# 30 of 34 token tiles transposed by VectorE and placed by transfers instead of TensorE transposes, in a hybrid FFN/convolution layer

## The chip, the cores and the metric

The kernel runs on the 8 cores of one Trainium2 chip. Each core computes one row of the batch (2048 prompt tokens) and 16 of the 128 sample tokens; the cores do not exchange data. The metric is the device time of the slowest core, in microseconds. Every row below is from core 0, the slowest one of the profiled execution.

## What is computed

One layer: a half-step SwiGLU feed-forward, a token mixer of two convolution groups, and a second half-step feed-forward, each followed by a layer norm.

```python
D_MODEL = 1024; SEQ = 2048; D_FF = 2816; K_A = 31; K_B = 3; D_IN = 5 * 512

def swiglu(x, w_gate, w_up, w_down):
    return (jax.nn.silu(x @ w_gate) * (x @ w_up)) @ w_down

x = layer_norm(ALPHA * x + 0.5 * swiglu(x, f1_wg, f1_wu, f1_wd), ln_f1_g, ln_f1_b)
z = x @ w_in + b_in
a_val, a_gate, g_b, g_c, b_val = jnp.split(z, 5, axis=-1)
ua = silu(layer_norm(causal_depthwise(a_val * sigmoid(a_gate), w_dw_a) + b_dw_a, ...))   # width 31
ub = g_b * causal_depthwise(g_c * b_val, w_dw_b)                                          # width 3
m = jnp.concatenate([ua, ub], axis=-1) @ w_o + b_o
x = layer_norm(ALPHA * x + m, ln_mix_g, ln_mix_b)
x = layer_norm(ALPHA * x + 0.5 * swiglu(x, f2_wg, f2_wu, f2_wd), ln_f2_g, ln_f2_b)
```

## The kernel before, in words

**Tiles and blocks.** The tokens lie in 17 tiles: 16 of 128 prompt tokens, and tile 16 with the 16 sample tokens. Tiles 0 to 7 are block 0, tiles 8 to 15 and 16 are block 1. The residual stream is token-major: a tile is 128 partitions (tokens) by 1024 features in f32, in one of the slots of `xr`, and it is spilled to DRAM between stages (`x1s` after the first feed-forward, `x2s` after the mixer). The input of a matmul that contracts over features must be feature-major: it lies in bf16 in `xA` (block 0) and `xB` (block 1), and `xcol(k, tok0, n)` is the 128 features of chunk k (of KC = 8) for n tokens. In the kernel before, tokens lie behind each other within a chunk.

**Stages.** `up` multiplies a block by gate and up weights: for each of 22 chunks of hidden width and each group of 512 (block 0) or 352 and 336 (block 1) tokens, `u_group` issues 16 matmuls (L563), ScalarE takes the silu into `sg`, and VectorE multiplies (L570) into `hT`. `down` works tile by tile: 44 matmuls (L627) from `hT`, then the residual and the layer norm on VectorE (L460 to L492) with a little GpSimd work in between. The mixer of a block is an in-projection (L720), gates (L782, L817), convolution (L838), and two units of four tiles (`unit_E`), each with a layer norm, an out-projection (L1003), the residual and the second layer norm. The program runs up(0, block 0), down(0, block 0), then up(0, block 1) merged with the mixer of block 0, down(0, block 1), up(1, block 0) merged with the mixer of block 1, down(1, block 0), up(1, block 1), down(1, block 1). In the merged stages `merge` takes the up groups as filler: after each piece of the mixer it issues as many up groups as the piece's number says, in an order fixed by these numbers.

**From token-major to feature-major.** When a tile's layer norm is done, its bf16 form stands in `xb` (2 slots). `xpose` transposes it: 8 matmuls of 128 x 128 against an identity (L438), a PSUM bank, and one copy by ScalarE (L442) into `xA` or `xB`. This happens 34 times: 17 times in `down(0, .)` for the mixer's input and 17 times in the units for the second feed-forward's.

```python
while len(pend) > (1 if late is None else 0) and not final:
    xpose(*pend.pop(0), tb())
```

**Queues and dependencies.** `Prog` (its class stands at L44 to L172) records each operation on its engine in program order, with what it reads and writes, and derives semaphore waits from these. Each engine's queue is in order, SyncE's too. SyncE issues the stores and loads of `xr` (`store_xr` L539, `load_xr` L419), the DRAM hops of the convolution (`uscr`, L799) and little else; GpSimd issues the weights (wgu, wd, win). `load_xr` reads, beside its source, what `gate[0]` names:

```python
gate = [()]
def load_xr(t, src, rtok=()):
    rtok = list(rtok) + list(gate[0])
    s = xrr()
    n = tok(t)[1]
    P.op("sp", lambda e: e.dma_start(out=xr[:n, s, :], in_=src), reads=list(rtok), writes=[("xr", s)],
         dma="xr_ld%d" % s)
```

From `down(0, block 0)` on the gate is `[("hT", 17, 1)]`: each load counts as a reader of that part of `hT`, so it waits for its last write, and its next write (by the multiply of chunk 17, group 1, of the following `up`) waits for all the loads issued before it.

## Time and profile before

| what | value |
|---|---|
| median of 3 runs | 1196.04 us (1195.96 to 1196.07) |
| the profiled execution's own time | 1196.45 us |
| its span, core 0 | 1194.9 us (cores 1192.1 to 1194.9) |
| granted TensorE clock | full in every slice |
| TensorE busy | 1179.9 us, 99% |
| VectorE busy | 599.8 us, 50% |
| ScalarE, GpSimd busy | 249.3 us (21%), 191.5 us (16%) |
| DMA | 155.92 MB, software queue 42.3% and hardware queue 22.7% of the 16 engines |

The stages of the profiled execution, in us from the span's start, with the busy time of TensorE and VectorE:

| stretch | stage | TensorE | VectorE |
|---|---|---|---|
| 0 to 170 | up(0, block 0) | 165.6 | 43.8 |
| 170 to 247 | down(0, block 0) | 77.0 | 46.0 |
| 247 to 521 | up(0, block 1) and mixer of block 0 | 272.7 | 161.2 |
| 521 to 603 | down(0, block 1) | 82.0 | 53.1 |
| 603 to 876 | up(1, block 0) and mixer of block 1 | 272.0 | 165.4 |
| 876 to 1195 | the second feed-forward's rest | 310.7 | 130.2 |

The span is the time between the first and the last record on the core; the execution's own time holds what lies around it. A busy share is an average over stages with different limits. A row with [x <-y] says that the engine stood x us before it and that y released it.

### The profile page before, as it was taken

Reading aid. Unit: us, or ns where it says so; the run is one execution under the profiler, and the core shown is the slowest. Engines: PE = TensorE matmul, PEld = TensorE weight load, DVE = VectorE, ACT = ScalarE, POOL = GpSimd, SP = SyncE. Lnnn points to the kernel's source line nnn. Section 1 sums busy time; section 2 is a strip of 40 time slices with the busy share of each in tenths; the row PEclk is TensorE's granted clock in tenths of the full one; section 3 lists DMA queues with packets and bytes.
Section 4 is the critical chain, followed back from the end, with each engine's and each line's share of the span. In section 5 each row is a group of like instructions: output and inputs, shape, how many; then the busy total and the mean of one; then the engine's idle time right before and its main releaser. Section 6 shows DMA issues by size and latency. Waiting matters only on the chain.

```text
span 1194.9 us, 20175 instructions; the slowest of 8 cores (1192.1 to 1194.9 us)
## 1 busy us (share of the span) xinstructions
PE 1179.9 (99%) x7240; PEld 644.0 (54%) x7240; DVE 599.8 (50%) x918; ACT 249.3 (21%) x451; POOL 191.5 (16%) x302
## 2 busy tenths in 40 slices
...
GB/s 281 114 211 139 142 143 152 150 153 121 120 102 112 131 129 165 200 184 124 105 114 117 114 108 125 120 135 185 185 163 136 76 107 86 71 72 89 28 105 105
DMA packets 70898, 155.92 MB, mean 130 GB/s; under 512 B 8912, under 2 KB 30608, under 8 KB 69760
## 3 DMA queue, kind: packets, MB, share of 16 engines
q0 software_dynamic: 31040, 76.07, 42.3%
q1 hardware_dynamic: 39760, 78.56, 22.7%
...
## 4 chain that ended last, share of the span: by engine, by line
PE 95%; DMA 2%; DVE 1%; issue 0%; ACT 0%; DVEq 0%; POOL 0%; SPq 0%; POOLq 0%; ACTq 0%
PE ps L563 50%; PE ps L627 25%; PE ps L720 11%; PE ps L1003 4%; PE ps L838 1%; DMA sb_xr<-x1s 1%; PE ps L438 1%; DMA sb_RW<-wgu 1%; PE ps L645 1%; PE ps L972 1%; PE ps L944 1%; DVE sb_RW L782 0%; PE ps L633 0%; DVE sb_RW L817 0%; DVE sb_ring L1179 0%
## 5 line engine op out<-in xcount | busy, mean ns | idle before, releaser
L563 PE MATMUL ps<-sb_xB,sb_ring 128*128 128x352 bf16 (+1 forms) x2112 | 319.6, 310 | 0.0
L563 PE MATMUL ps<-sb_xA,sb_ring 128*128 128x512 bf16 (+1 forms) x1472 | 311.6, 370 | 2.0 <-DVE sb_ring L1179 2.0
L570 DVE TENSOR_TENSOR sb_hT<-sb_sg,ps 128x352 bf16<-128x352 f32 (+3 forms) x224 | 129.6, 579 | 348.9 <-PE ps L563 323.3
L627 PE MATMUL ps<-sb_RW,sb_hT 128*128 128x512 bf16 x1364 | 297.0, 379 | 0.0
L563 PEld LDWEIGHTS ps<-sb_xB,sb_ring 128*128 128x128 bf16 x2112 | 205.8, 98 | 106.7 <-issue 1.1
L563 PEld LDWEIGHTS ps<-sb_xA,sb_ring 128*128 128x128 bf16 x1472 | 142.9, 98 | 156.9 <-issue 4.5
L627 PEld LDWEIGHTS ps<-sb_RW,sb_hT 128*128 128x128 bf16 x1364 | 132.9, 98 | 158.1 <-issue 0.2
L568 ACT ACTIVATE sb_sg<-ps 128x352 f32<-128x352 f32 (+3 forms) x224 | 113.8, 508 | 489.2 <-PE ps L563 454.0
L376 POOL DMA_DIRECT2D sb_ring<-wgu x84 | 46.6, 555 | 463.2 <-PE ps L563 406.7
L460 DVE SCALAR_TENSOR_TENSOR sb_xr<-sb_xr,ps 128x1024 f32<-128x1024 f32 x47 | 57.3, 1218 | 94.2 <-PE ps L627 77.0
L468 POOL TENSOR_SCALAR sb_mv<-sb_mv 128x1 f32<-128x1 f32 (+1 forms) x50 | 43.5, 869 | 354.4 <-DVE sb_mv L466 347.3
L720 PE MATMUL ps<-sb_xB,sb_wring 128*128 128x512 bf16 (+2 forms) x480 | 73.8, 310 | 0.5 <-DVE sb_RW L782 0.4
L720 PE MATMUL ps<-sb_xA,sb_wring 128*128 128x512 bf16 x320 | 73.0, 379 | 0.0
L464 DVE BATCH_NORM_STATS2 sb_stt<-sb_xr 128x6 f32<-128x512 f32 (+1 forms) x100 | 64.3, 685 | 5.1
L720 PEld LDWEIGHTS ps<-sb_xB,sb_wring 128*128 128x128 bf16 x480 | 46.7, 98 | 26.6 <-issue 1.6
L479 DVE SCALAR_TENSOR_TENSOR sb_xr<-sb_xr,sb_mv,sb_lnb 128x1024 f32<-128x1024 f32 (+1 forms) x33 | 42.4, 1284 | 18.5 <-POOL sb_mv L470 16.0
L720 PEld LDWEIGHTS ps<-sb_xA,sb_wring 128*128 128x128 bf16 x320 | 31.3, 98 | 34.4
L782 DVE SCALAR_TENSOR_TENSOR sb_RW<-ps,sb_cst,sb_RW 128x512 bf16<-128x512 f32 (+2 forms) x24 | 41.7, 1779 | 7.0 <-PE ps L720 5.9
L817 DVE SCALAR_TENSOR_TENSOR sb_RW<-ps,sb_cst,sb_RW 128x512 bf16<-128x512 f32 (+1 forms) x20 | 39.8, 2069 | 7.2 <-PE ps L720 7.1
L476 DVE SCALAR_TENSOR_TENSOR sb_xr<-sb_xr,sb_mv,sb_lnb 128x1024 f32<-128x1024 f32 (+1 forms) x33 | 42.2, 1280 | 1.7
L389 POOL DMA_DIRECT2D sb_wring<-win x40 | 22.0, 553 | 121.2 <-PE ps L720 119.8
L442 ACT ACTIVATE sb_xB<-ps 128x1024 bf16<-128x1024 bf16 (+1 forms) x18 | 16.8, 941 | 114.3 <-PE ps L438 114.2
...
## 6 DMA issues: line engine op xcount, KB each, us to landing
sb_ring<-wgu POOLq DMA_DIRECT2D x84, 512.0 KB, 8.1
sb_RW<-wd POOLq DMA_DIRECT2D x33, 512.0 KB, 11.1
...
sb_RW<-uscr SPq DMA_DIRECT2D x128, 67.0 KB, 5.5
sb_xr<-xp SPq DMA_DIRECT2D x16, 512.0 KB, 9.4
x1s<-sb_xr SPq DMA_DIRECT2D x16, 512.0 KB, 4.0
sb_xr<-x1s SPq DMA_DIRECT2D x16, 512.0 KB, 11.5
x2s<-sb_xr SPq DMA_DIRECT2D x16, 512.0 KB, 8.0
```

The lines of the kernel that those rows point to most:

```text
L376: P.op("pool", lambda e, q=q: e.dma_start(out=ring[:, s, q * m:(q + 1) * m], in_=wgu[w][f][:, q * m:(q + 1) * m], max_dma_last_dim=8192), ...
L460: P.op("dve", lambda e: e.scalar_tensor_tensor(out=xr[:n, s, :], in0=xr[:n, s, :], scalar=in_scale, in1=add, op0=ALU.mult, op1=ALU.add), r ...
L464: P.op("dve", lambda e, h=h: e.bn_stats(out=stt[:n, m, h, :], in_=xr[:n, s, h * 512:(h + 1) * 512]), reads=[("xr", s)], writes=[("stt", m, ...
L468: P.op("pool", lambda e: e.tensor_scalar(out=mv[:n, m, 3:4], in0=mv[:n, m, 1:2], scalar1=eps, scalar2=None, op0=ALU.add), reads=[("mv", m) ...
L476: P.op("dve", lambda e: e.scalar_tensor_tensor(out=xr[:n, s, :], in0=xr[:n, s, :], scalar=mv[:n, m, 0:1], in1=lnb[:n, 0, :], op0=ALU.subtr ...
L479: P.op("dve", lambda e: e.scalar_tensor_tensor(out=xr[:n, s, :], in0=xr[:n, s, :], scalar=mv[:n, m, 2:3], in1=lnb[:n, 1, :], op0=ALU.mult, ...
L563: ins = e.matmul(bank(bk, n), lhsT=ring[:, s, c:c + 128], rhs=xcol(k, tok0, n), start=(k == 0), stop=(k == KC - 1))
L568: P.op("act", lambda e: e.activation(out=sg[:, q, :n], in_=bank(bg, n), func=AF.Silu), reads=pst(bg), writes=[("sg", q)])
L570: P.op("dve", lambda e: e.tensor_tensor(out=hT[:, f, l0:l0 + n], in0=sg[:, q, :n], in1=bank(bu, n), op=ALU.mult), reads=[("sg", q)] + pst( ...
L627: ins = e.matmul(ps[:n, (yb + h) * 512:(yb + h + 1) * 512], lhsT=hT[:, f, l0:l0 + n], rhs=wd[:, f, h * 512:(h + 1) * 512], start=(f == 0), ...
L720: ins = e.matmul(bank(bk, n), lhsT=wring[:, slot, k * 128:(k + 1) * 128], rhs=xcol(k, tok0, n), start=(k == 0), stop=(k == KC - 1))
L1003: ins = e.matmul(ps[:n, (4 + h) * 512:(5 + h) * 512], lhsT=lhs(k), rhs=wo[:, k, h * 512:(h + 1) * 512], start=(k == 4), stop=(k == 3))
```

## The change

Of the 34 transposes, 30 go another way: tiles 0 to 6 and 8 to 14 in `down(0, .)`, and the 16 prompt tiles in the units. The last prompt tile of each block in `down(0, .)` and tile 16 (twice) keep `xpose` (L434 in the new file). For the 30:

- VectorE transposes the tile in blocks of 32 x 32 (L447), all 128 blocks in one instruction, from `xb` to `tq` (2 slots). After that each 32 x 32 block is transposed within itself, but stands on the partitions it came from.
- SyncE issues four writes from `tq` to `xscr` in DRAM (L451; 64 KB each, 4 slots of `xscr`), which put the blocks into the right rows. A write moves pieces of 512 bytes.
- `land_moves`, called later in the order, issues one transfer from `xscr` into `xA` or `xB` (L454; 256 KB in rows of 2 KB), which waits for the four writes.

For pieces of 512 bytes the feature-major buffers have another layout: runs of 16 tokens, and within a run of tokens the 8 feature chunks. A matmul's moving operand so becomes runs of 32 bytes, 256 bytes apart. The host's `xta` and `xtb` are laid out in that way. In `down`, a tile's transposes no longer stand between two tiles' matmuls. `dynamic_dma_scratch_size=8192` gives the software queue's descriptors less room than before.

```diff
-    nc = bass.Bass("TRN2", target_bir_lowering=False)
+    nc = bass.Bass("TRN2", target_bir_lowering=False, dynamic_dma_scratch_size=8192)
+    xscr = nc.dram_tensor("xscr", [4, 128, D], BF16).ap()
-        xA = sb("xA", [128, 4, KC, 256], BF16)
-        xB = sb("xB", [128, KC, NTOK - BLK], BF16)
+        xA = sb("xA", [128, KC * BLK], BF16)
+        xB = sb("xB", [128, KC * (NTOK - BLK)], BF16)
+        tq = sb("tq", [128, 2, D], BF16)
+        def xall(tok0, n):
+            (buf, o) = (xA, tok0) if tok0 < BLK else (xB, tok0 - BLK)
+            return buf[:, o * KC:(o + n) * KC]
+
         def xcol(k, tok0, n):
...
+            return xall(tok0, n).rearrange("p (b k l) -> p k b l", k=KC, l=16)[:, k, :, :]
+        moves = []
+
+        def xmove(t, c):
+            s, d = tqr(), xsr()
+            P.op("dve", lambda e: e.transpose(out=tq[:, s, :].rearrange("p (q h k l) -> p k q h l", q=4, h=2, k=KC),
+                                              in_=xb[:, c, :].rearrange("p (k q h l) -> p k q h l", q=4, h=2, k=KC)),
+                 reads=[("xb", c)], writes=[("tq", s)])
+            for a in range(4):
+                P.op("sp", lambda e, a=a: e.dma_start(out=xscr[d].rearrange("(q i) (a c) -> a i q c", q=4, a=4)[a],
+                                                      in_=tq[32 * a:32 * a + 32, s, :].rearrange("i (q c) -> i q c", q=4)),
+                     reads=[("tq", s)], writes=[("xscr", d, a)], dma="xw%d_%d" % (s, a))
+            moves.append(lambda: P.op("sp", lambda e: e.dma_start(out=xall(t * 128, 128), in_=xscr[d]),
+                                      reads=[("xscr", d, a) for a in range(4)], writes=[("xT", t)], dma="xm%d" % d))
+
+        def land_moves():
+            while moves:
+                moves.pop(0)()
@@ down
-                while len(pend) > (1 if late is None else 0) and not final:
+                land_moves()
+                while pend:
                     xpose(*pend.pop(0), tb())
...
+                        if t < 16 and i < len(tl) - 1:
+                            xmove(t, c)
+                            return []
+                        return [(t, c)]
@@ unit_E, B(i)
+                land_moves()
                 for k in at(i, 5, True):
-                    xpose(tl[k], xbs[k], ((3, 3, 3, 7), (3, 6, 3, 7))[par][k])
+                    xmove(tl[k], xbs[k])
```

Three places of the order, in which a number behind x counts equal neighbours and "waits" names what an instruction waits for. First TensorE in `down(0, block 0)`, before. Rows of L627 are the down matmuls, rows of L438 a tile's transposes.

```order
L627 MATMUL ps<-sb_RW,sb_hT 128x512 x132
L438 MATMUL ps<-sb_ident_bf,sb_xb 128x128 x8
L627 MATMUL ps<-sb_RW,sb_hT 128x512 x44
L438 MATMUL ps<-sb_ident_bf,sb_xb 128x128 x8
L627 MATMUL ps<-sb_RW,sb_hT 128x512 x44
L438 MATMUL ps<-sb_ident_bf,sb_xb 128x128 x8
```

The same place after, where L641 are the down matmuls, L577 the up matmuls, L738 the in-projection and L434 the transposes:

```order
L641 MATMUL ps<-sb_RW,sb_hT 128x512 x352
L577 MATMUL ps<-sb_xB,sb_ring 128x352 x32
L577 MATMUL ps<-sb_xB,sb_ring 128x336 x16
L738 MATMUL ps<-sb_xA,sb_wring 128x512 x16
L577 MATMUL ps<-sb_xB,sb_ring 128x352 x16
L434 MATMUL ps<-sb_ident_bf,sb_xb 128x128 x8
```

The 352 matmuls of the eight tiles now follow each other with nothing between, and only tile 7's transposes are left, behind the first piece of the in-projection.

Second, SyncE's queue in the first unit of the mixer of block 1, before. L539 is a store of a finished tile (two rows of the same store instruction read alike), L419 a load of the next tile's x1s; `xr_st1` is the store that frees slot 1.

```order
L539 DMA x2s<-sb_xr 128x1024 [waits S_dve] x2
L419 DMA sb_xr<-x1s 128x1024 [waits xr_st0]
L539 DMA x2s<-sb_xr 128x1024 [waits S_dve] x2
L419 DMA sb_xr<-x1s 128x1024 [waits xr_st1,S_act]
L419 DMA sb_xr<-x1s 128x1024 [waits xr_st2,S_act]
```

The same place after. L553 and L415 are that store and that load, L451 the writes to `xscr` (the four of a tile are a row and its "x3"), L454 the transfer from `xscr`; `xw1_0` to `xw1_3` are the four writes from slot 1 of `tq`.

```order
L553 DMA x2s<-sb_xr 128x1024 [waits S_dve]
L415 DMA sb_xr<-x1s 128x1024 [waits xr_st1,S_act]
L454 DMA sb_xB<-xscr 128x1024 [waits xw1_0,xw1_1,xw1_2,xw1_3]
L451 DMA xscr<-sb_tq 32x4x256 [waits xm0,S_dve]
L451 DMA xscr<-sb_tq 32x4x256 x3
L454 DMA sb_xB<-xscr 128x1024 [waits xw0_0,xw0_1,xw0_2,xw0_3]
L451 DMA xscr<-sb_tq 32x4x256 [waits xm1,S_dve]
L451 DMA xscr<-sb_tq 32x4x256 x3
L415 DMA sb_xr<-x1s 128x1024 [waits xr_st2,S_act]
```

The load into slot 2, which stood directly behind the one into slot 1, now has two transfers from `xscr`, each with its wait for writes, and two tiles' writes between.

Third, VectorE at that place, before: L570 is the multiply of an up group, L918 to L921 are statistics of the convolution's layer norm.

```order
L570 TENSOR_TENSOR sb_hT<-sb_sg,ps 128x512 [waits S_act,S_pe] x4
L918 BN_STATS sb_sttc<-ps 128x6 [waits S_pe]
L919 BN_AGGR sb_mvc<-sb_sttc 128x2 [waits S_dve]
L921 TENSOR_SCALAR sb_mvc<-sb_mvc 128x1 [waits S_dve]
L570 TENSOR_TENSOR sb_hT<-sb_sg,ps 128x512 [waits xr_ld0,xr_ld1,xr_ld2,S_act,S_pe]
```

After, where L584 is that multiply and L447 the block transpose:

```order
L584 TENSOR_TENSOR sb_hT<-sb_sg,ps 128x512 [waits S_act,S_pe] x2
L447 STREAM_TRANSPOSE sb_tq<-sb_xb 128x8x8x16 [waits xw0_0,xw0_1,xw0_2,xw0_3]
L584 TENSOR_TENSOR sb_hT<-sb_sg,ps 128x512 [waits S_act,S_pe]
L447 STREAM_TRANSPOSE sb_tq<-sb_xb 128x8x8x16 [waits xw1_0,xw1_1,xw1_2,xw1_3]
L584 TENSOR_TENSOR sb_hT<-sb_sg,ps 128x512 [waits S_act,S_pe]
...
L584 TENSOR_TENSOR sb_hT<-sb_sg,ps 128x512 [waits xr_ld0,xr_ld1,xr_ld2,S_act,S_pe]
```

Two block transposes now stand between the multiplies, each waiting for the writes of the tile two before it, and the multiply that waits for the three loads is still there.

## Rows read from the trace of the kernel before

**Rows 1.** The page: busy time by engine; the last chain by engine and by line.

```profile
PE 1179.9 (99%) x7240; PEld 644.0 (54%) x7240; DVE 599.8 (50%) x918; ACT 249.3 (21%) x451; POOL 191.5 (16%) x302
...
PE 95%; DMA 2%; DVE 1%; issue 0%; ACT 0%; DVEq 0%; POOL 0%; SPq 0%; POOLq 0%; ACTq 0%
PE ps L563 50%; PE ps L627 25%; PE ps L720 11%; PE ps L1003 4%; PE ps L838 1%; DMA sb_xr<-x1s 1%; PE ps L438 1%; DMA sb_RW<-wgu 1%; PE ps L645 1%; PE ps L972 1%; PE ps L944 1%; DVE sb_RW L782 0%; PE ps L633 0%; DVE sb_RW L817 0%; DVE sb_ring L1179 0%
```

**Rows 2.** The last chain in order of time: start, duration (us), engine, line, count.

```profile
197.67 9.50 PE ps L627 x44
...
207.61 9.50 PE ps L627 x44
```

**Rows 3.** Groups by form, whole run: xcount | busy us, mean ns | idle before, releaser.

```profile
L438 PE MATMUL ps<-sb_ident_bf,sb_xb 128*128 128x128 bf16 x256 | 19.2, 219 | 0.0
...
L489 DVE SCALAR_TENSOR_TENSOR sb_xb<-sb_xr,sb_mv,sb_lnb 128x1024 bf16<-128x1024 f32 x16 | 20.5, 1284 | 13.6 <-POOL sb_mv L470 13.3 <-DVE sb_xr L486 0.3
...
L782 DVE SCALAR_TENSOR_TENSOR sb_RW<-ps,sb_cst,sb_RW 128x512 bf16<-128x512 f32 x12 | 30.5, 2541 | 6.1 <-PE ps L720 5.9
...
L1179 DVE CAST sb_xA<-sb_RW 128x1024 bf16<-128x1024 f32 x3 | 2.1, 691 | 6.8 <-DMA sb_RW<-xta 6.8
```

**Rows 4.** Timeline, mixer of block 0: start, duration (us), engine, line, operation.

```profile
461.52 16.70 SPq L419 DMA_DIRECT2D sb_xr<-x1s  x3
...
476.71 0.52 DVE L570 TENSOR_TENSOR sb_hT<-sb_sg,ps 128x352 bf16<-128x352 f32 x1 [7.61 <-DMA sb_xr<-x1s]
...
478.19 2.55 PE L563 MATMUL ps<-sb_xB,sb_ring 128*128 128x352 bf16 x16
```

**Rows 5.** Line L419 (loads of x1s), 814.5 to 820 and 834 to 836.

```profile
L419 SPq DMA_DIRECT2D sb_xr<-x1s x2: 635/977/1319, 814.1 to 815.6; - x2
...
DMA to landing us min/median/max: 15.4/17.0/18.6
...
L419 SPq DMA_DIRECT2D sb_xr<-x1s x1: 320/320/320, 835.2 to 835.2; - x1
...
DMA to landing us min/median/max: 10.7/10.7/10.7
```

**Rows 6.** Timeline, mixer of block 1, first unit.

```profile
806.03 0.61 PE L438 MATMUL ps<-sb_ident_bf,sb_xb 128*128 128x128 bf16 x8
...
821.62 0.61 PE L438 MATMUL ps<-sb_ident_bf,sb_xb 128*128 128x128 bf16 x8
...
834.18 3.62 PE L563 MATMUL ps<-sb_xA,sb_ring 128*128 128x512 bf16 x16
...
834.40 0.69 DVE L570 TENSOR_TENSOR sb_hT<-sb_sg,ps 128x512 bf16<-128x512 f32 x1 [4.90 <-PE ps L972]
```

**Rows 7.** Timeline of VectorE, down(0, block 1): the first instruction of two tiles.

```profile
545.71 1.21 DVE L460 SCALAR_TENSOR_TENSOR sb_xr<-sb_xr,ps 128x1024 f32<-128x1024 f32 x1
...
553.50 1.21 DVE L460 SCALAR_TENSOR_TENSOR sb_xr<-sb_xr,ps 128x1024 f32<-128x1024 f32 x1
```

**Rows 8.** Line L799 (loads from uscr): whole run, 312 to 320, 620 to 628.

```profile
L799 SPq DMA_DIRECT2D sb_RW<-uscr x128: 302/432/1665, 270.2 to 740.9; - x128
...
DMA to landing us min/median/max: 2.9/2.9/2.9
...
DMA to landing us min/median/max: 7.2/8.2/9.2
```

**Rows 9.** Queues, 460 to 470, then 806 to 812: packets, MB, share of 16 engines.

```profile
q0 software_dynamic: 474, 1.17, 86.3%
q1 hardware_dynamic: 150, 0.56, 16.1%
...
q0 software_dynamic: 324, 0.80, 82.5%
q1 hardware_dynamic: 6, 0.02, 0.7%
...
x2s<-sb_xr SPq DMA_DIRECT2D x1, 512.0 KB, 8.4
```

More of the change, by code:

```diff
@@ L325, in build_nc @@
         xbr = Rot(range(2))
+        tqr = Rot(range(2))
+        xsr = Rot(range(4))
         mvr = Rot(range(4))
@@ L346, in xtoks @@
             return [("xT", t) for t in range(NT) if tok(t)[0] < tok0 + n and tok(t)[0] + tok(t)[1] > tok0]
+        def xall(tok0, n):
+            (buf, o) = (xA, tok0) if tok0 < BLK else (xB, tok0 - BLK)
+            return buf[:, o * KC:(o + n) * KC]
         def xcol(k, tok0, n):
-            if tok0 >= BLK:
-                return xB[:, k, tok0 - BLK:tok0 - BLK + n]
-            (p, o) = divmod(tok0, 256)
-            if o + n <= 256:
-                return xA[:, p, k, o:o + n]
-            assert o == 0 and n == 512
-            return xA[:, p:p + 2, k, :]
-        def xall(tok0, n):
-            if tok0 >= BLK:
-                return xB[:, :, tok0 - BLK:tok0 - BLK + n]
-            (p, o) = divmod(tok0, 256)
-            return xA[:, p, :, o:o + n]
+            return xall(tok0, n).rearrange("p (b k l) -> p k b l", k=KC, l=16)[:, k, :, :]
         RMS = ["RMC", "RM5", "RM6", "RM7", "RM8"]
@@ L442, in xpose_from @@
             P.op("act", lambda e: e.activation(
-                out=xall(tok0, n),
-                in_=psb[:, bk * 1024: bk * 1024 + KC * n].rearrange("p (k n) -> p k n", k=KC), func=AF.Identity),
+                out=xall(tok0, n).rearrange("p (b k l) -> p k b l", k=KC, l=16),
+                in_=psb[:, bk * 1024: bk * 1024 + KC * n].rearrange("p (k b l) -> p k b l", k=KC, l=16), func=AF.Identity),
                 reads=pst(bk), writes=[("xT", t)])
+        moves = []
[13 more added lines that the diff above has]
+                moves.pop(0)()
         def quarter_gather(bk):
@@ L685, in fin_tail @@
                         store_xr(t, slots[i], prow(yp, t) if t < 16 else ys[:, :])
-                        return None
+                        return []
                 if t == 16:
@@ L692, in down @@
                     ctx = ln_head(t, slots[i], pairs[i], in_scale, eps)
-                    return pend, lambda: pend.append(fin_tail(i, ctx))
-                pend.append(fin(i))
+                    return pend, lambda: pend.extend(fin_tail(i, ctx))
+                pend.extend(fin(i))
                 if late is not None:
-                    pend.append(fin(*late))
+                    pend.extend(fin(*late))
                     late = None
@@ L1116, in four @@
             def four():
+                land_moves()
                 n = len(ub.items)
@@ L1156, in fetch_xt @@
             t0, n, src = (BLK + 512 * j, 512, xtb[j]) if j < 2 else (SEQ, NS, xts)
-            P.op("pool", lambda e: e.dma_start(out=xall(t0, n), in_=src.rearrange("p (k n) -> p k n", k=KC)),
+            P.op("pool", lambda e: e.dma_start(out=xall(t0, n), in_=src),
                  writes=xtoks(t0, n), dma="xt%d" % j)
@@ L1184, in build_nc @@
         for i in range(4):
-            first.append(staged(2 * i, xta[i], xA[:, i, :, :].rearrange("p k n -> p (k n)"),
+            first.append(staged(2 * i, xta[i], xall(256 * i, 256),
                    (["xTh%d" % i], xtoks(256 * i, 256))))
```

5 lines of the change are left out of this document (2 added, 3 removed).

## The prediction

> **What bounds the kernel now.** I read the page first: TensorE is busy 1179.9 of 1194.9 us and holds 95% of the chain that ended last [rows 1]. So what leaves TensorE's queue shortens the run, as long as nothing else becomes late, and what makes TensorE wait lengthens it at once. The chain in order of time shows what a tile's transposes cost between two tiles of a down projection: the 44 matmuls start at 197.67 and last 9.50 us, the next 44 start at 207.61, so 0.44 us lie between [rows 2]. The groups by form give 219 ns for one such transpose [rows 3], but they overlap; eight of them take 0.44 us of the path.
>
> Then I asked where TensorE's cover is thin, and read the timelines of the two mixers. In the mixer of block 0 VectorE stood 7.61 us in front of one multiply (476.71) until a load of x1s landed [rows 4]; this load had been issued at 461.52. The load does not feed the multiply. `load_xr` names hT (17,1) as read (`gate`), so the next write of hT (17,1) waits for all loads issued before it. The reader is to see that TensorE took its next up group at 478.19, right behind. The mixer of block 1 has the same place: two loads issued at 814.1 and 815.6 landed within 18.6 us [rows 5], the later one at 834.2, and the multiply started at 834.40, while TensorE had begun the next group at 834.18 [rows 6]. (The row puts the wait down to PE; the load's landing fits to 0.2 us.) The second half of this group, 1.8 us on at 836.0, is what needs the bank, and the multiply ended at 835.1: slack 0.9 us. Whatever makes these two loads later than that stops VectorE and then TensorE.
>
> **What the change removes.** 30 of 34 tiles lose their 8 transposes: 30 x 0.44 = 13.2 us off TensorE's path [rows 2], 14 tiles in the down projections (6.2 us) and 16 in the mixers (7.0 us). ScalarE's eviction goes too; ScalarE is not on the path [rows 1], nothing counted. Fewer bytes per partition for the software queue's descriptors, the new layout of the loads and the changed source of the x transfers: nothing, bounds below.
>
> **What it adds on VectorE.** One block transpose per tile, 128x1024 bf16 with 32-byte runs out. The trace has none. Nearest rows: a cast of as many elements, 0.69 us; a plain pass over 1024, 1.28; a write with a step of two elements, 2.54 for 512, so 5.1 for 1024 [rows 3]. The runs are 16 elements long, nearer to the plain pass; I take 1.2. In a down projection VectorE needs 7.8 us for a tile (545.71 to 553.50) [rows 7] and would need 9.0, while TensorE takes 9.5: hidden, and it stays hidden up to 1.7 us. The Trainium skill (VectorE: DVE Perf Modes, "The three transpose paths") gives 311 ns for 128x128 bf16 on VectorE; eight of these would be an estimated 2.5 us. No row shows one.
>
> **What it adds on SyncE and the queues.** Per tile four writes to xscr (W, 512 packets of 512 B, 0.25 MB) and, after they have landed, one transfer back (M, 0.25 MB). SyncE's queue is in order. M waits for W, and the next tile's W, the stores and the loads stand behind M. An issue takes 0.43 us [rows 8], so W costs 1.7. How long W takes to land from its last issue, L, no row shows. Nearest are the 67 KB loads from uscr, 536-byte packets too: 2.9 us at best, 7.2 to 9.2 at worst [rows 8]. The rows of the queues say which end to take: while the software queue held 82.5% and 86.3% of the engines (wd and wgu loads), the hardware queue moved 6 packets in 6 us and 150 in 10 us [rows 9]. These are stretches of the two mixers. I take L = 7, range 2.9 to 9.2. The Trainium skill (DMA: Bandwidth & Descriptors, "Queues, rings and completion order") says that an engine goes round-robin between the rows it has work for. By that rule W would get its turn soon and L would be near its low end; the 6 packets of [rows 9] speak against it, since a store of 512 KB was issued in that stretch and took 8.4 us to land.
>
> In the down projections a tile comes every 9.5 us, L + 1.7 + 0.4 = 9.1, and nothing there waits on xT soon: no cost.
>
> Mixer of block 1, first unit. The four tiles come within 15.6 us (806.03 to 821.62) [rows 6], and SyncE would need 3 x 9.1 = 27.3. In the new order W, M, W, M, W, M, W stand before the load into slot 2. From 806.0: W1 out 807.7, M1 814.7, W2 out 816.8, M2 823.8, W3 out 825.9, M3 832.9, W4 out 835.0, then the load at 835, which was issued at 815.6. A load issued at 835.2 landed in 10.7 us [rows 5], so it lands at 845.7 instead of 834.2: 11.5 late, less 0.9 slack: 10.6. Three of the removed transposes lie inside this chain and give nothing: 1.3. **Loss 11.9.**
>
> Mixer of block 0, first unit. Only W1, M1, W2 stand ahead of the load; SyncE gets to it about 1.8 us later than 461.52 (W2's issues). But 0.5 MB more are in the queue ahead of it, and that queue moved 0.56 MB in 10 us [rows 9]: between 0 and 9 us, I take 5. 6.8 late, less 1.0 slack (the multiply ended at 477.2, TensorE went on at 478.19 [rows 4]), plus 1.3 of savings within: **loss 7.1.**
>
> The second units end without such a gate. Their last tiles come about as close together as the first unit's, two of them some 4 us apart, and each transpose waits for the W of two tiles before (tq has 2 slots), which stands behind an M: VectorE stands some 9.1 - 4 = 5 us, of which I let free banks cover 2 to 3. Bounds 0 to 5; I take 3 for block 0, 1 for block 1 (one up group is left there).
>
> **Sum**: -13.2 + 11.9 + 7.1 + 3 + 1 = +9.8 us. The profiled execution took 1196.45 (span 1194.9), the median is 1196.04, 0.4 less; so 1206. With L at 2.9 and no more queueing the load in block 1 goes out at 806.0 + 3 x 5.0 + 1.7 = 822.7 and lands, with 10.7, at 833.4, in time; the other terms shrink to 2: 1185. With L at 9.2 it goes out at 841.6 and lands with 18.6 at 860, 26 late; 9 + 1.8 in block 0; 6 for the rest: about 1225.
>
> **Rivals.** (1) *The gain stays*: W lands within 3 to 4 us, TensorE keeps its cover, 1185 to 1193. For it: the 2.9 us of [rows 8], and stores that the stalled TensorE's software queue makes room for. Against: [rows 9]. It decides at L about 4.5, where the losses are 13. By the skill's round-robin rule this is the case. Chance 0.26. (2) *They cancel* within 0.2% (2.4 us, about what a measurement tells from no change): 0.08. (3) *VectorE becomes the bound*: at 2.5 us a tile needs 10.3 against 9.5, 14 x 0.8 = 11 us on top of the stalls, about 1217; at 5.1 us 14 x 3.4 = 48, over 1240. Or the 32-byte runs slow the up matmuls: L563 and L720 hold 61% of the chain [rows 1], so 2% would be 15 us. No row has a moving operand in short runs. Together 0.09. (4) *The change does nothing* is out: the transposes leave the queue. (5) The forecast, SyncE's order and the gate cost more than the transposes: 0.57.
>
> Slower 0.57 + 0.09 = 0.66, same 0.08, faster 0.26. The range 1187 to 1220 leaves out the best half of the first rival's low end and the worst of the bound cases; the forecast's own range is 1199 to 1220.
>
> **What would show it.** Right: 32 transposes left on PE; 30 on VectorE of 1.0 to 1.6 us; W landing in 6 to 9 us in the mixers; SyncE waiting on DMA xscr some 7 us each; a wait of VectorE's multiply on the load of x1s of over 12 us in each mixer, and idle time of TensorE near it, about 10 us in block 1. Down projections at 9.50 us a tile without gaps. Wrong: up matmuls longer than before in the same form; W landing in under 4.5 us; TensorE's idle in the mixers unchanged.

## The result

The changed kernel is slower: 1241.54 us against 1196.05, ratio 1.038 with a 95% interval of 1.0348 to 1.0413. Times of whole kernels are medians of the executions in which no die showed a lower clock (here three, 1238.55 to 1244.77; a fourth took 1270.33). The prediction had slower as the likeliest case, but said 1206 with a range of 1187 to 1220, and the result lies above it. The profiled execution took 1241.54 us with a span of 1240.0 on its slowest core.

The page of the kernel after: busy time, and the last chain by engine and by line, as in [rows 1].

```profile
PE 1180.8 (95%) x7000; PEld 634.0 (51%) x7000; DVE 633.6 (51%) x948; ACT 220.4 (18%) x421; POOL 186.7 (15%) x302
...
PE 81%; DMA 10%; DVE 4%; SPq 2%; issue 2%; POOL 1%; DVEq 0%; ACT 0%; POOLq 0%; ACTq 0%
PE ps L577 44%; PE ps L641 19%; PE ps L738 10%; DMA xscr<-sb_tq 6%; PE ps L1021 4%; DMA sb_xr<-x1s 2%; PE ps L856 1%; SPq L451 1%; DMA sb_RW<-xta 1%; DVE sb_xr L474 1%; PE ps L659 1%; DVE sb_stt L478 1%; DVE sb_tq L447 1%; POOL sb_mv L482 1%; DVE sb_xb L503 1%
...
L447 DVE STREAM_TRANSPOSE sb_tq<-sb_xb 128x1024 bf16<-128x1024 bf16 x30 | 37.2, 1239 | 30.0 <-DMA xscr<-sb_tq 30.0
```

TensorE has 240 matmuls fewer than in [rows 1] and is as busy as before, and it stands 59.2 us of the span in place of 15.0. The writes to `xscr` now hold 6% of the chain. A block transpose takes 1.239 us.

**By stage.** The first and the last down matmul of each projection in TensorE's timeline cut both runs into the same stages. Before: 168.6, 78.4, 273.9, 81.4, 274.1, 76.5, 155.0, 87.0 us. After: 167.3, 76.1, 293.6, 93.2, 291.8, 76.5, 155.0, 86.4. So 19.7 us came in up(0, block 1) with the mixer of block 0, 11.8 in down(0, block 1) and 17.7 in up(1, block 0) with the mixer of block 1. Down(0, block 0) gave 2.3 us back, and the rest is as before within 1.3. In what follows M0 and M1 are the two merged stages and D1 is down(0, block 1).

**TensorE's stalls.** All rows of TensorE's timeline of the kernel after with a wait of more than 1 us, from 170 us on:

```profile
264.38 6.31 PE L738 MATMUL ps<-sb_xA,sb_wring 128*128 128x512 bf16 x16 [5.20 <-DMA sb_xA<-xscr]
486.96 4.85 PE L577 MATMUL ps<-sb_xB,sb_ring 128*128 128x352 bf16 x16 [6.32 <-DVE sb_hT L584]
521.63 6.02 PE L577 MATMUL ps<-sb_xB,sb_ring 128*128 128x336 bf16 x40 [1.68 <-DVE sb_hT L584]
531.87 5.31 PE L577 MATMUL ps<-sb_xB,sb_ring 128*128 128x352 bf16 x24 [4.21 <-DVE sb_hT L584]
598.58 0.36 PE L434 MATMUL ps<-sb_ident_bf,sb_xb 16*128 16x16 bf16 x8 [11.30 <-DVE sb_xb L503]
867.93 1.09 PE L990 MATMUL ps<-sb_ident,sb_wring 128*128 128x128 f32 x4 [8.55 <-ACT sb_wring L980]
882.57 3.57 PE L1021 MATMUL ps<-sb_wo,sb_RW 128*128 128x512 bf16 x8 [9.25 <-DVE sb_xr L474]
```

That is 46.5 us in seven places. Two were in the prediction (486.96 and 882.57, the gate), and 521.63 and 531.87 belong to its second unit of block 0. It had none at the start of M0 (264.38), none for tile 16 in D1 (598.58), and none in the first unit of block 1 ahead of the gate (867.93). A row names only the last engine of a chain: at 867.93 TensorE waits for ScalarE, which waited for GpSimd, which waited for VectorE, and VectorE's own row says why.

The timeline of VectorE and SyncE in the mixer of block 1, after:

```profile
861.48 1.25 DVE L447 STREAM_TRANSPOSE sb_tq<-sb_xb 128x1024 bf16<-128x1024 bf16 x1 [12.98 <-DMA xscr<-sb_tq]
...
872.98 2.29 SPq L451 DMA_DIRECT2D xscr<-sb_tq  x4
875.42 0.34 SPq L415 DMA_DIRECT2D sb_xr<-x1s  x1
...
880.60 0.69 DVE L584 TENSOR_TENSOR sb_hT<-sb_sg,ps 128x512 bf16<-128x512 f32 x1 [14.99 <-DMA sb_xr<-x1s]
```

And the chain in order of time there, three writes of `xscr`, each from its last issue to its landing:

```profile
834.28 7.35 DMA xscr<-sb_tq
...
844.48 16.91 DMA xscr<-sb_tq
...
863.24 9.18 DMA xscr<-sb_tq
```

VectorE stood 12.98 us for a slot of `tq` and then 14.99 for the load of x1s, which SyncE issued at 875.4 behind these writes. Before, the two loads left at 814.1 and 815.6 [rows 5].

**The clock.** The windows of the kernel after: in each row the busy times, then the granted clock, the DMA share and GB/s.

```profile
264.00:268.00 4.00, 3.62 (x9) 1.31 (x10) 0.00 (x0) 0.00 (x0) 0.00 (x0) 0.50 0.93 371
271.00:280.00 9.00, 9.00 (x53) 5.01 (x52) 6.30 (x10) 1.60 (x3) 1.06 (x2) 1.00 0.99 171
880.00:884.00 4.00, 1.43 (x4) 0.58 (x5) 3.20 (x6) 0.00 (x0) 0.00 (x0) 0.50 0.07 12
884.00:888.00 4.00, 4.00 (x12) 1.40 (x10) 3.26 (x4) 0.00 (x0) 1.60 (x3) 0.54 0.57 137
888.00:892.00 4.00, 4.00 (x21) 1.81 (x19) 2.72 (x4) 0.60 (x1) 0.10 (x1) 1.00 0.99 188
```

Behind these two stalls TensorE runs at 0.50, its lower level of 1.2 GHz, for about 5 us: 12 matmuls fit in 884 to 888 where 21 fit in the 4 us behind. Busy time should have fallen by 13.2 us and rose by 0.9, so this costs 14.1 us. The windows agree: from 170 us on the stretches at 0.50 hold 27.3 us of busy time, half of which is 13.7. So stalls of 44.2 us more than before are paid as 58.

### The profile page after: what moved, and what is told of

Its sections match the earlier page's. It is cut to its first block, busy times and chain, and to the rows that moved or that the text cites. A ratio compares the mean times of both kernels' runs of the same rounds, so it can differ in the third digit from the quotient of the medians.

```text
span 1240.0 us, 20098 instructions; the slowest of 8 cores (1228.0 to 1240.0 us)
## 1 busy us (share of the span) xinstructions
PE 1180.8 (95%) x7000; PEld 634.0 (51%) x7000; DVE 633.6 (51%) x948; ACT 220.4 (18%) x421; POOL 186.7 (15%) x302
## 4 chain that ended last, share of the span: by engine, by line
PE 81%; DMA 10%; DVE 4%; SPq 2%; issue 2%; POOL 1%; DVEq 0%; ACT 0%; POOLq 0%; ACTq 0%
PE ps L577 44%; PE ps L641 19%; PE ps L738 10%; DMA xscr<-sb_tq 6%; PE ps L1021 4%; DMA sb_xr<-x1s 2%; PE ps L856 1%; SPq L451 1%; DMA sb_RW<-xta 1%; DVE sb_xr L474 1%; PE ps L659 1%; DVE sb_stt L478 1%; DVE sb_tq L447 1%; POOL sb_mv L482 1%; DVE sb_xb L503 1%
## 5 line engine op out<-in xcount | busy, mean ns | idle before, releaser
L577 PE MATMUL ps<-sb_xB,sb_ring 128*128 128x352 bf16 (+1 forms) x2112 | 323.2, 313 | 12.7 <-DVE sb_hT L584 12.2
L577 PE MATMUL ps<-sb_xA,sb_ring 128*128 128x512 bf16 (+1 forms) x1472 | 311.7, 371 | 1.0 <-DVE sb_ring L1199 0.7
L584 DVE TENSOR_TENSOR sb_hT<-sb_sg,ps 128x352 bf16<-128x352 f32 (+3 forms) x224 | 129.3, 578 | 333.9 <-PE ps L577 300.2
L641 PE MATMUL ps<-sb_RW,sb_hT 128*128 128x512 bf16 x1364 | 298.4, 381 | 0.0
L577 PEld LDWEIGHTS ps<-sb_xB,sb_ring 128*128 128x128 bf16 x2112 | 207.2, 98 | 124.2 <-issue 15.6
L577 PEld LDWEIGHTS ps<-sb_xA,sb_ring 128*128 128x128 bf16 x1472 | 143.5, 98 | 158.7 <-issue 4.8
L641 PEld LDWEIGHTS ps<-sb_RW,sb_hT 128*128 128x128 bf16 x1364 | 133.8, 98 | 162.3 <-issue 4.1
L372 POOL DMA_DIRECT2D sb_ring<-wgu x84 | 46.5, 554 | 462.6 <-PE ps L577 412.8
L738 PE MATMUL ps<-sb_xA,sb_wring 128*128 128x512 bf16 x320 | 75.7, 389 | 5.2 <-DMA sb_xA<-xscr 5.2
L738 PE MATMUL ps<-sb_xB,sb_wring 128*128 128x512 bf16 (+2 forms) x480 | 73.9, 310 | 0.6 <-DVE sb_RW L800 0.4
L738 PEld LDWEIGHTS ps<-sb_xB,sb_wring 128*128 128x128 bf16 x480 | 46.7, 98 | 26.9 <-issue 1.8
L738 PEld LDWEIGHTS ps<-sb_xA,sb_wring 128*128 128x128 bf16 x320 | 31.9, 100 | 41.9 <-issue 9.2
L447 DVE STREAM_TRANSPOSE sb_tq<-sb_xb 128x1024 bf16<-128x1024 bf16 x30 | 37.2, 1239 | 30.0 <-DMA xscr<-sb_tq 30.0
L385 POOL DMA_DIRECT2D sb_wring<-win x40 | 22.1, 555 | 128.1 <-PE ps L738 126.7
```

The lines of the kernel that those rows point to most:

```text
L372: P.op("pool", lambda e, q=q: e.dma_start(out=ring[:, s, q * m:(q + 1) * m], in_=wgu[w][f][:, q * m:(q + 1) * m], max_dma_last_dim=8192), ...
L447: P.op("dve", lambda e: e.transpose(out=tq[:, s, :].rearrange("p (q h k l) -> p k q h l", q=4, h=2, k=KC), in_=xb[:, c, :].rearrange("p (k ...
L577: ins = e.matmul(bank(bk, n), lhsT=ring[:, s, c:c + 128], rhs=xcol(k, tok0, n), start=(k == 0), stop=(k == KC - 1))
L584: P.op("dve", lambda e: e.tensor_tensor(out=hT[:, f, l0:l0 + n], in0=sg[:, q, :n], in1=bank(bu, n), op=ALU.mult), reads=[("sg", q)] + pst( ...
L641: ins = e.matmul(ps[:n, (yb + h) * 512:(yb + h + 1) * 512], lhsT=hT[:, f, l0:l0 + n], rhs=wd[:, f, h * 512:(h + 1) * 512], start=(f == 0), ...
L738: ins = e.matmul(bank(bk, n), lhsT=wring[:, slot, k * 128:(k + 1) * 128], rhs=xcol(k, tok0, n), start=(k == 0), stop=(k == KC - 1))
```

## The experiments

Each is timed in alternation with the kernel before on the same chip. M0, D1 and M1 are of the slowest core of its profiled execution (before: 273.9, 81.4, 274.1; after: 293.6, 93.2, 291.8). e1, e12, e14, e16 and e17 do not compute the layer: e1 and e12 leave transfers out, and the other three leave the blocks of the moved tiles in wrong rows.

| run | median us | ratio to before (95%) | M0 | D1 | M1 |
|---|---|---|---|---|---|
| e1 no moves | 1202.31 | 1.0045 (1.0028, 1.0062) | 273.3 | 91.1 | 272.6 |
| e2 layout only | 1196.34 | 0.9991 (0.998, 1.0001) | 274.2 | 81.2 | 274.4 |
| e3 tile 16 later | 1244.01 | 1.0386 (1.0371, 1.0402) | 299.2 | 88.2 | 293.1 |
| e4 transfer back later | 1232.93 | 1.0297 (1.028, 1.0314) | 288.1 | 90.7 | 288.0 |
| e5 no gate | 1237.58 | 1.0338 (1.031, 1.0366) | 296.2 | 93.6 | 282.1 |
| e6 before, no gate | 1195.24 | 0.9978 (0.9969, 0.9988) | 272.6 | 81.4 | 274.1 |
| e7 down only | 1208.72 | 1.0089 (1.0068, 1.0109) | 282.3 | 90.3 | 273.2 |
| e8 mixers only | 1240.80 | 1.0365 (1.0349, 1.038) | 293.3 | 90.0 | 290.7 |
| e9 down only, tile 16 later | 1204.64 | 1.0049 (1.0033, 1.0066) | 282.7 | 80.6 | 278.5 |
| e10 e9, later transfer, no gate | 1198.43 | 1.0007 (0.9997, 1.0017) | 273.4 | 80.6 | 279.7 |
| e11 all waits relaxed | 1220.45 | 1.0186 (1.017, 1.0202) | 284.4 | 90.4 | 280.0 |
| e12 writes only | 1230.62 | 1.0266 (1.025, 1.0283) | 289.0 | 90.1 | 284.9 |
| e13 e11, writes on ScalarE | 1215.74 | 1.0147 (1.0133, 1.0161) | 288.7 | 87.1 | 274.0 |
| e14 e11, one coarse write | 1206.21 | 1.007 (1.0054, 1.0085) | 272.9 | 92.6 | 274.8 |
| e15 only down(0, block 0), 7 tiles | 1194.13 | 0.9975 (0.9964, 0.9986) | 276.3 | 81.2 | 274.2 |
| e16 e11, four coarse writes | 1206.42 | 1.0082 (1.0066, 1.0098) | 276.6 | 92.6 | 272.2 |
| e17 changed, one coarse write | 1231.18 | 1.0283 (1.0268, 1.0297) | 281.7 | 97.9 | 287.9 |
| e18 only down(0, block 0), 6 tiles | 1192.30 | 0.9957 (0.9943, 0.9972) | 272.1 | 81.4 | 274.0 |

M0 is a loose measure once the transfers are in. The eight cores of one execution run the same program; in the kernel before their M0 lies between 272.6 and 274.6 us, in the kernel after between 281.5 and 293.6 (mean 287.8), in e3 between 283.7 and 300.1, in e5 between 285.0 and 300.5. M1 lies between 287.9 and 291.8 after. So some 5 us of difference in M0 between two of these kernels is not read as the work of an edit.

**Is it the transfers, VectorE or the layout? (e1, e2)**

```diff
@@ e1: xmove keeps only the transpose on VectorE
-            for a in range(4):
-                P.op("sp", ... out=xscr[d]..., in_=tq[32 * a:32 * a + 32, s, :]...)
-            moves.append(lambda: P.op("sp", ... out=xall(t * 128, 128), in_=xscr[d] ...))
@@ e2: the kernel before with xA and xB in runs of 16 and dynamic_dma_scratch_size=8192
```

> The four writes to xscr and the transfer back are left out for the 30 tiles, so xA and xB keep old contents there; the 30 block transposes on VectorE, the layout, the order and everything else stay. Theory A (the loss comes from SyncE's queue standing on the writes, and with it late loads, late transposes and late transfers): the two merged stages fall from 293.7 and 291.8 us to about 270 each, only the 11 us of down(0, block 1) stay, total about 1196. Rival V (VectorE's 37 us of block transposes are the bound): the merged stages stay above 285, total above 1225.

> The kernel before with only the layout in runs of 16 tokens and the smaller descriptor space; all 34 transposes stay on TensorE. Theory A: no change, 1195 to 1197.5, matmuls of L563 at 310 and 370 ns as before. Rival R (moving operands in 32-byte runs cost TensorE time, or the smaller descriptor space makes GpSimd's loads late): over 1200.

e2 is as fast as the kernel before, so short runs of the moving operand and the smaller descriptor space cost nothing. e1 takes M0 and M1 back to 273.3 and 272.6: the transfers cost 20.3 and 19.2 us there. It leaves D1 at 91.1, so VectorE and the order make 9.7 of its 11.8 us alone. It also shows that the transposes taken out of the two merged stages hardly came back: 0.6 and 1.5 us. These are 8.8 us, 20 tiles at 0.44: the mixers' 16, and tiles 5, 6, 13 and 14, whose transposes stood behind the last down matmul of their projection. TensorE stands 4.8 and 3.8 us in these two stages of e1, in place of 1.3 and 1.0, so other waits had taken the room. e1 was forecast at 1196 and took 1202.31.

**D1: tile 16 and VectorE (e3, e7, e8, e9)**

```diff
@@ e3, and in e9
-                while pend:
+                while pend and not (pend[0][0] == 16 and i < 6):
                     xpose(*pend.pop(0), tb())
@@ e7 and e9: the units' tiles on TensorE (e8: down's tiles on TensorE, in the order before)
-                    xmove(tl[k], xbs[k])
+                    xpose(tl[k], xbs[k], ((3, 3, 3, 7), (3, 6, 3, 7))[par][k])
```

> Of the changed kernel only the order of tile 16's transposes in down(0, block 1) is changed: one tile later on TensorE, as in the kernel before. Theory A (TensorE's 11.3 us before them are a wait for VectorE's tile 16, made by the new place in the order): that stage falls from 93.2 to about 81 us, the total by 10 to 13 us, to about 1231. Rival (the stage is late because VectorE is late on all its tiles with 8.9 us each): the wait moves to the next tile and the total falls by under 4 us.

> Of the 30 moved tiles only the 14 in the down projections are moved; the 16 in the mixers stay on TensorE. From the stages of the changed kernel: down(0, block 0) 76.1 instead of 78.4, 5 to 9 us of wait at the start of the mixer of block 0, down(0, block 1) 91 to 93 instead of 81.4, the rest as before: total 1208 to 1214. If the down projections' moves also cause the stalls late in the merged stages, over 1220.

> Only the 16 tiles in the mixers are moved; the down projections keep TensorE's transposes in the order of the kernel before. Theory A: down(0, block 1) goes back to about 81.5, the merged stages keep all but the 5 to 9 us at their start: 286 and 291, total 1225 to 1230. With e7 the two parts' losses should add to the whole 47 us within 5; if they do not, one part's lateness feeds the other.

> e7 (only the 14 tiles of the down projections moved) with tile 16's transposes one tile later on TensorE, as in the kernel before. In e3 this order was tried in a stage that was late for another reason. Theory O (the order alone makes the 9 us in down(0, block 1) when nothing else is late): the stage falls from 90.3 to 81 to 83, total about 1201. Theory V (VectorE is the bound there with nine tiles at 8.9 us in place of 7.8): the stage stays at 87 or more, total over 1206.

In the kernel before, tile 16's transposes stand behind the 44 matmuls of tile 13; with `while pend` they stand one tile earlier, behind tile 12's. VectorE's timeline in D1 of the kernel after, the first instruction of two tiles:

```profile
565.27 1.18 DVE L474 SCALAR_TENSOR_TENSOR sb_xr<-sb_xr,ps 128x1024 f32<-128x1024 f32 x1
...
574.19 1.18 DVE L474 SCALAR_TENSOR_TENSOR sb_xr<-sb_xr,ps 128x1024 f32<-128x1024 f32 x1
```

A tile takes VectorE 8.9 us, 1.1 more than in [rows 7]. For tile 16 it needs nearly as long as for another, while TensorE spends 2.6 us on its 88 small matmuls. So VectorE falls behind TensorE over this stage, and tile 16's `xb` was ready 11.30 us after TensorE wanted it.

e3 missed: 1231 was forecast and it took 1244.01, no less than the changed kernel. D1 falls only to 88.2, and M1 rises by 1.3. In that kernel VectorE enters D1 late from M0. e8 shows this: with all transposes of D1 back on TensorE it is still 90.0 (82.5 to 90.5 over the cores), and VectorE stands 22.9 us for a load of xp there. On the cleaner base of e7 the order does count: D1 falls from 90.3 to 80.6, but M1 rises from 273.2 to 278.5. So more than half of it is only handed on. In TensorE's timeline of e9 (the first row in D1, the second at the head of M1):

```profile
588.57 1.67 PE L641 MATMUL ps<-sb_RW,sb_hT 128*128 128x512 bf16 x7 [1.42 <-DVE sb_xr L474]
...
621.65 1.01 PE L434 MATMUL ps<-sb_ident_bf,sb_xb 128*128 128x128 bf16 x8 [3.57 <-DVE sb_xb L503]
```

D1 and M1 together: 363.5 in e7, 359.1 in e9, 355.5 in the kernel before with its 3.1 us of transposes. So the order costs 4.4 us and moving the seven tiles 359.1 - 352.4 = 6.7. I put this down to VectorE's block transposes: e9 has the transfers too, but e7 with them and e1 without any have the same D1 (90.3 and 91.1). The parts do not add: e7 loses 0.9% and e8 3.65%, together more than the 3.8% of the whole change, and D1 is late in either.

**The waits (e4, e5, e6, e11, e12)**

```diff
@@ e4 (e11: keep=2)
-        def land_moves():
-            while moves:
+        def land_moves(keep=1):
+            while len(moves) > keep:
@@ e5, e6 (in the kernel before), e10, e11, e13 to e16, e18
-        gate[0] = [("hT", 17, 1)]
@@ e11: besides e4, e5 and e3
-        tq = sb("tq", [128, 2, D], BF16)
+        tq = sb("tq", [128, 4, D], BF16)
@@ e12: the changed kernel without the transfer back (moves.append)
```

> The transfer from xscr of a tile is issued one tile later, behind the writes of the next tile, so that SyncE seldom waits for writes; at the ends of the stages all are issued. Theory A (it is the in-order wait on SyncE): waits of SyncE on writes fall from 138.7 us to under 40, the merged stages lose 25 to 35 of their 44 us of stalls, total 1207 to 1218. Rival Q (the writes themselves are slow to land, and the bytes on the queues make loads and transposes late, whatever SyncE does): total stays above 1230.

> The changed kernel without the gate: loads of xr no longer count as readers of hT (17,1), so the multiply of that group waits for no load. Theory A, part gate (the late loads hurt mainly through this multiply, in which VectorE stood 22.0 us in two places): the merged stages fall by 6 to 12 us together, total 1230 to 1236. Rival (the tile's own residual addition waits for the same load a little later, and the loads start at other times): within 3 us of 1243.

> The kernel before without the gate. It has 7.61 and 4.9 us of VectorE's wait there, hidden from TensorE. If the gate only keeps order, no change within 2 us, 1195 to 1198; if it spreads the loads over time, slower by 2 us or more.

> The changed kernel, all 30 tiles moved, with four slots of tq in place of two, the transfers from xscr two tiles later, no gate, and tile 16 later. No wait of SyncE or VectorE for writes should be left in the mixers. Theory A (the waits make the loss): the merged stages fall to 272 to 277, total 1190 to 1200. Rival Q (the bytes, packets and issues of the moves delay the loads of x1s and the weights, whatever waits): the merged stages stay above 283, total over 1212.

> The changed kernel with the four writes per tile, but the transfer from xscr into xA or xB left out (they keep old contents for the 30 tiles), so SyncE waits for no write; VectorE still waits for the writes when it takes a slot of tq again. Theory A (SyncE's wait in front of the transfer): merged stages near 276. Rival (VectorE's wait for its slots and the writes' own slowness): merged stages above 284. e1, without the writes too, had 273.3 and 272.6.

The waits of SyncE on writes to `xscr` (total, times, longest), after, in e4 and in e11:

```profile
SPq L154 <- DMA xscr<-sb_tq: 138.7, 91, 9.6
```

```profile
SPq L154 <- DMA xscr<-sb_tq: 60.4, 38, 6.4
```

```profile
SPq L154 <- DMA xscr<-sb_tq: 12.8, 9, 4.3
```

SyncE's waits go, but only a part of the loss goes with them. e4 wins 0.8%, where 1207 to 1218 had been expected; e11, with no gate and four slots as well, wins 1.9% and still has 284.4 and 280.0. In e12 SyncE waits for no write at all, and the merged stages are at 289.0 and 284.9; VectorE still waits 25.3 us there for slots of `tq` (30.0 in the changed kernel). My theory of SyncE's wait falls as the only cause. The gate costs 9.7 us in M1 and none can be read in M0 (e5). Of the whole run e5 gains 0.4%, and its interval overlaps the changed kernel's. In the kernel before the gate costs 0.2% (e6).

**The queue and the pieces (e13, e14, e16, e17)**

```diff
@@ e13: e11 with
-                P.op("sp", lambda e, a=a: e.dma_start(out=xscr[d]...
+                P.op("act", lambda e, a=a: e.dma_start(out=xscr[d]...
@@ e14 (on e11) and e17 (on the changed kernel); e16 the same rows in four writes of 32 partitions
-            for a in range(4): ... 128 pieces of 512 bytes each
+            P.op("sp", lambda e: e.dma_start(out=xscr[d], in_=tq[:, s, :]), ...)
```

> e11 with the four writes of a tile issued by ScalarE in place of SyncE, so that no load of x1s stands behind a write on SyncE and no slow issue of a write (1.5 to 3.4 us each in e11) holds SyncE. Theory S (SyncE's one queue, backed up with writes, makes the loads late): the merged stages fall from 284.4 and 280.0 to 278 or less each, total under 1212. Rival D (the 16 engines have no room left for the bytes and packets, whichever queue): within 3 us of e11's 1221. ScalarE then stands on its own issues, and the silu of an up group behind it comes up to 2 us later.

> e11 with one write per tile in rows of 2 KB in place of four writes in pieces of 512 bytes: the same bytes, a quarter of the packets and of the issues; the 32x32 blocks are then not put into their places, so the output of the moved tiles is wrong. Theory P (the 512-byte pieces and the four issues are the cost): the merged stages fall below 278 each, total about 1203 to 1208. Rival B (the bytes and one more transfer in each direction in a full queue are the cost): within 4 us of e11.

> e11 with four writes per tile as there, each of 32 rows of 2 KB in place of 128 pieces of 512 bytes; the 32x32 blocks are not put into their places, so the output of the moved tiles is wrong. Theory P1 (the 512-byte pieces are the cost): as e14, merged stages 272 to 276, total 1204 to 1208. Rival P2 (four issues instead of one): as e11, 280 or more, total 1216 or more.

> The changed kernel itself with nothing relaxed (two slots of tq, transfer back at once, gate, tile 16's place), but one write per tile in rows of 2 KB; output of the moved tiles wrong as in e14. If the in-order wait of SyncE is the root, it stays though the pieces are gone: total above 1225. If the wait is only as long as slow pieces make it: merged stages 276 to 282, total 1208 to 1218.

The queues from 460 to 475 us, the same place of the mixer of block 0, in e11 (packets, MB, share of 16 engines):

```profile
q0 software_dynamic: 851, 1.91, 90.3%
q1 hardware_dynamic: 563, 0.30, 9.4%
```

and in e14:

```profile
q0 software_dynamic: 696, 1.60, 71.3%
q1 hardware_dynamic: 431, 1.29, 29.1%
```

Both queues have transfers outstanding here. For each packet of the software queue the hardware queue gets 0.66 packets in e11 and 0.62 in e14, though they are of 0.5 KB in the one and 3 KB in the other; so in e11 it moves a quarter of the bytes. The ratio is not a constant. In the next 15 us of e11 it is 1.0, and in the same two stretches of the changed kernel 1.3 and 1.6:

```profile
q0 software_dynamic: 725, 1.87, 74.8%
q1 hardware_dynamic: 722, 1.21, 30.6%
...
q0 software_dynamic: 629, 1.48, 64.3%
q1 hardware_dynamic: 805, 0.99, 21.7%
...
q0 software_dynamic: 752, 1.67, 65.2%
q1 hardware_dynamic: 1177, 1.65, 36.2%
```

The Trainium skill (DMA: Bandwidth & Descriptors, "Queues, rings and completion order") says that an engine goes round-robin between the rows at the granularity of a packet. Its packet drains some 9 to 17 descriptors, while the rows count pieces of 0.5 and 3 KB one by one, so they do not test the rule itself. The first two pairs of rows look like a turn that is counted in pieces and not in bytes, and then small pieces lose by it, while I had cited the rule for a short L. The ratios from 0.62 to 1.6 show that this is not the whole of it. That the pieces cost time is shown below (e14, e16); by which mechanism is not.

The loads of x1s stand behind in the same queue. Line L451 in e11, 468 to 482 us, and the load issued next:

```profile
L451 SPq DMA_DIRECT2D xscr<-sb_tq x4: 1512/2794/3407, 469.4 to 477.0; - x4
...
DMA to landing us min/median/max: 26.8/30.6/31.4
...
480.18 0.65 SPq L415 DMA_DIRECT2D sb_xr<-x1s  x1
```

The issues themselves took 1.5 to 3.4 us in place of 0.43, and the writes landed 27 to 31 us later. In e14 the timeline has that load 11.4 us earlier, of which 1.0 is the whole unit's (its writes before stand at 458.38, in e11 at 459.38):

```profile
468.83 0.34 SPq L415 DMA_DIRECT2D sb_xr<-x1s  x1
```

e16 keeps four issues and has coarse rows; it is as fast as e14. So it is the pieces, not the number of issues. e17 has coarse rows and all the waits: 281.7 and 287.9, and 1231.18 in all, as expected for waits that stay though the pieces are gone (above 1225). The four corners, as M0 + M1 and the ratio of the whole run:

| | pieces of 512 bytes | rows of 2 KB |
|---|---|---|
| waits as changed | 585.4, 1.0380 (after) | 569.6, 1.0283 (e17) |
| waits relaxed | 564.4, 1.0186 (e11) | 547.7, 1.0070 (e14) |

In the merged stages of the slowest cores waits cost about 21.5 us and pieces about 16 us, and together they are the 37.4 us by which these stages grew. The whole run gives the pieces less: coarse rows win 1.0 and 1.2%, which is 12 to 14 us, and relaxed waits 1.9 and 2.1%, 23 to 25 us. A part of what e17 and e14 win in the mixers comes back in D1, 97.9 against 93.2 and 92.6 against 90.4. By the whole run each costs about this with or without the other. As the mean of the eight cores the pieces cost 8.8 us of M0 + M1 with the waits and 14.2 without, so the split is not sharper than that. "Waits" are all four edits of e11 together, tile 16's place among them.

e13 puts the writes on ScalarE, small pieces and all. M1 is then at 274.0, so there all that e11 still lost came from having the writes in SyncE's queue with the loads. Whether it is their place ahead of the loads is not separated from the queue of their own that the trace gives them. M0 is at 288.7: TensorE waits for ScalarE's silu, which stands behind the issues, as in the row

```profile
524.14 6.17 PE L577 MATMUL ps<-sb_xB,sb_ring 128*128 128x336 bf16 x31 [4.69 <-ACT sb_sg L582]
```

**What is left that pays (e10, e15, e18)**

```diff
@@ e10: e9 + e4 + e5.  e15: e4 + e5, the units on TensorE, and (e18: len(tl) - 2)
-                        if t < 16 and i < len(tl) - 1:
+                        if b == 0 and i < len(tl) - 1:
```

> e9 with the transfers from xscr one tile later (as in e4) and without the gate. Expected sum: 1196.6 less 1.3 to 2.6 (the gate, e6), less 14 x 0.44 = 6.2 (the transposes), plus what is left of the wait at the start of the mixer of block 0 (7.8 us in e7, 3 in e4): 1190 to 1194, faster than the kernel before. Rival: VectorE's share in down(0, block 1) and the wait for the last tile keep it at 1196 or more.

> Only tiles 0 to 6 in down(0, block 0) are moved, the other 27 tiles stay on TensorE; transfers one tile later and no gate as in e10. VectorE is not short in that stage (eight tiles, none of 16 tokens). Sum: the gate's 0.2%, minus 2.3 us of that stage, plus 1.6 to 3 us of wait for the last tile's transfer: between 0.2% and 0.35% faster than the kernel before, about equal to e6. If VectorE's share is not what cost e10 its gain, it will be no faster than e10 (1.0007).

> e15 with tile 6 on TensorE too, so that the last transfer lands before the in-projection asks for its tile (e15: 2.56 us of wait and a slow start of TensorE behind it on the slowest core). Stage down(0, block 0) 76.4, the merged stage 273: 1192.5 to 1194.5 beside 1197.9 of the kernel before, ratio 0.996; if the wait was not what held e15, no better than e15 (0.9975).

e10 missed: 1190 to 1194 was forecast and it only equals the kernel before, as VectorE's lateness eats the gain (D1 and M1 together 360.3 in place of 355.5). e15 and e18 move nothing there and are faster. The page of e18, and its wait of SyncE on writes:

```profile
PE 1177.3 (99%) x7192; PEld 641.4 (54%) x7192; DVE 607.3 (51%) x924; ACT 243.4 (20%) x445; POOL 191.0 (16%) x302
```

```profile
SPq L154 <- DMA xscr<-sb_tq: 0.5, 2, 0.3
```

e18 is the fastest version: 0.43% faster than the kernel before. About half of it is the gate's (e6: 0.22%), and the rest, 2.5 us, answers to the six tiles' 6 x 0.44 = 2.6. Five of them stood inside down(0, block 0), which takes 76.1 us in e18 and 78.4 in e6. The intervals of e6 and e18 overlap by a little, and they were not timed side by side, so that second half is likely, not certain.

## Why the prediction was wrong

The sign and the chain were right: SyncE's in-order queue, the gate and the late loads of x1s. What failed is the sum, which took +9.8 us where the profiled executions differ by 45.1. Two of its steps were wrong in kind: the down projections were put at nothing ("hidden", "no cost") and cost 11.1 and 8.4 us in the runs with the moves only there. The rest are terms that were too small or missing. By its terms:

- **Removed, -13.2.** Inside down(0, block 0) the five tiles whose transposes stood there give their 2.2 us back in full (2.3). In the merged stages e1 gives back 2.1 of 8.8 us, for other waits take the room. The prediction had 14 tiles in the down projections, but four of them had their transposes in the merged stages.
- **Block transpose, 1.2 us.** Measured 1.239. The rival with 2.5 us (an estimate from the Trainium skill, VectorE: DVE Perf Modes, "The three transpose paths", eight times 311 ns) is out by the row of L447: the 128 blocks of 32x32 of eight chunks take half of that in one instruction.
- **"While TensorE takes 9.5: hidden."** Wrong in D1. The comparison was of one tile with one tile, where the stage has nine tiles for VectorE, one of which takes TensorE 2.6 us. With the seven moved tiles it costs 6.7 us (e9), and the new place of tile 16's transposes, which I did not read in the order, 4.4 more.
- **"Nothing there waits on xT soon: no cost."** Wrong at the end of down(0, block 0). With win, wo and wgu loading, a write took up to 13.1 us to land, SyncE stood in front of the transfer, and the last tile's writes left 8 us late. The in-projection waited 5.20 us. In e7, which has it too, M0 is 8.4 us longer on the slowest core (on another core 2 us shorter), and e10, with the transfer one tile later, has M0 at 273.4.
- **Block 1, +11.9 and +1; block 0, +7.1 and +3.** Undersized: M1 and M0 grew by 17.7 and 19.7, that is 22.1 and 24.1 with the ten tiles' transposes that left each (4.4), and of the latter some 8.4 are the term above. L was 7.4, 16.9 and 9.2 us in the chain, not 7, and the high end of 9.2 had been taken from loads of 536-byte packets in shorter trains. VectorE's wait for a slot of `tq`, priced only for the second units, came in the first one too (12.98 us). And the sum had no term for the small pieces beyond L, which hold the issues of SyncE and the loads behind them: 1.0 to 1.2% of the run (e14, e17).
- **The clock.** No term stood for it; it is 14.1 us, a quarter of what the stalls cost on the slowest core. The trace of before has nearly no stall to read it from.
- **The rivals.** The gain stays: excluded. VectorE as the bound: true in D1 alone. Short runs of the moving operand: excluded by e2.

My first explanation after the result, that SyncE's waits make all of the loss, was a part of it at most: e11, e14 and e17 split the 3.8% into some 2% of waits (SyncE's, VectorE's and the gate's, with tile 16's place), 1.0 to 1.2% of small pieces, and 0.7% that e14 keeps, with D1 at 92.6. No run relaxes VectorE's wait for `tq` alone, so the 2% are not split further. Not settled is what an issue of L451 stood for in the 3.4 us.
